# A hybrid attention and state-space layer on one core: convolution steps spread over the attention units, low parts of the weights on the vector engine, panels loaded a tile earlier

## The reference

```
proj  = RMSNorm(x) @ W_in              # q, k, v, forget logits, z, xBC, dt, two gates
att   = softmax(q k^T * scale + c_q - c_k, causal) v      # 16 heads x 64
xBC   = silu(causal convolution of width 4 over time (xBC) + bias)   # 4096 channels
y_ssm = Mamba-2 scan(xBC, dt) * silu(z), grouped RMSNorm
x     = x + (sigmoid(g_att) * (att @ W_pa) + sigmoid(g_ssm) * (y_ssm @ W_pb)) @ W_out
x     = x + relu(RMSNorm(x) @ W_up)^2 @ W_down
```

## Time and profile before

| what | value |
|---|---|
| median of 3 runs | 2886.76 us (2885.06 to 2887.47) |
| profiled execution | 2885.89 us, its span 2884.1 us |
| mean granted TensorE clock | 0.978 |
| PE busy | 2737.1 us, 95% |
| DVE busy | 1577.2 us, 55% |
| ACT busy | 1022.4 us, 35% |
| POOL busy | 405.7 us, 14% |

### The profile page before, as it was taken

How to read it: one execution, slowest core, us unless ns; L and a number is a source line. 1 busy time by engine, 2 the same in 40 slices (tenths; PEclk the granted TensorE clock), 3 DMA queues, 4 the chain that set the end, 5 groups by cost and what they waited for, 6 DMA issues and landing times. The chain is left out here.

```text
span 2884.1 us, 47789 instructions
## 1 busy us (share of the span) xinstructions
PE 2737.1 (95%) x18754; PEld 2658.0 (92%) x18754; DVE 1577.2 (55%) x2867; ACT 1022.4 (35%) x2353; POOL 405.7 (14%) x475
## 2 busy tenths in 40 slices
PE   6998979999999999997999989998989999999999
PEld 5997978989999889887999979998989999999999
DVE  4336337656566565565898864464373444434434
ACT  4223336556666655653434331121231111111110
POOL 0000012212122222222555520000000000000000
PEclk8999999999999999998999999999989999999999
DMA  3222232132232222215888873343221111111112
GB/s 115 90 90 53 79 90 91 43 101 76 67 108 76 66 93 58 84 63 140 205 194 214 201 203 121 112 134 128 65 99 58 45 44 45 44 45 44 48 67 96
DMA packets 334448, 273.31 MB, mean 95 GB/s; under 512 B 95952, under 2 KB 311632, under 8 KB 334096
## 3 DMA queue, kind: packets, MB, share of 16 engines
q1 hardware_dynamic: 334224, 270.25, 32.9%
HBM read 197.90 MB, written 72.28 MB: 94 GB/s over the span
## 5 line engine op out<-in xcount | busy, mean ns | idle before, releaser
L411 PE MATMUL banks<-w_hi,xn_hi 128*128 128x256 f32 x1440 | 407.8, 287 | 8.7 <-DVEq L368 5.0
L411 PE MATMUL banks<-w_lo,xn_hi 128*128 128x256 f32 x1440 | 405.5, 286 | 0.0
L414 PE MATMUL banks<-xn_hi,w_hi 128*128 128x352 f32 x1152 | 379.5, 329 | 0.7 <-ACT att_xs L986 0.7
L414 PE MATMUL banks<-xn_hi,w_lo 128*128 128x352 f32 x1152 | 378.7, 329 | 0.0
L414 PE MATMUL banks<-xn_lo,w_hi 128*128 128x352 f32 x1152 | 378.2, 328 | 0.0
L411 PE MATMUL banks<-w_hi,xn_lo 128*128 128x256 f32 x1280 | 366.3, 286 | 0.0
L411 PEld LDWEIGHTS banks<-w_hi,xn_hi 128*128 128x128 f32 x1440 | 276.7, 192 | 10.6 <-DVEq L368 5.1
L411 PEld LDWEIGHTS banks<-w_lo,xn_hi 128*128 128x128 f32 x1440 | 276.6, 192 | 0.2
L1704 PE MATMUL banks<-h_hi,w_hi 128*128 128x352 f32 x768 | 248.8, 324 | 1.9 <-DVEq L1625 1.9
L1704 PE MATMUL banks<-h_lo,w_hi 128*128 128x352 f32 x768 | 248.6, 324 | 0.0
L1704 PE MATMUL banks<-mlp_uhi,w_hi 128*128 128x352 f32 x768 | 248.6, 324 | 0.0
(11 more groups left out here) (293 smaller groups left out, 6160.8 us busy)
## 6 DMA issues: line engine op xcount, KB each, us to landing
w_raw<-in_w_in SPq DMA_DIRECT2D x44, 1024.0 KB, 5.5
scratch_xbc<-att_co SPq DMA_DIRECT2D x32, 512.0 KB, 2.6
ssd_ab<-scratch_acum SPq DMA_DIRECT2D x64, 256.0 KB, 6.0
br_g<-scratch_gates SPq DMA_DIRECT2D x72, 176.0 KB, 2.8
scratch_gates<-hand_tanh SPq DMA_DIRECT2D x48, 176.0 KB, 5.4
scratch_z<-att_z_stage SPq DMA_DIRECT2D x64, 128.0 KB, 1.9
ssd_xbc<-scratch_xbc SPq DMA_DIRECT2D x64, 128.0 KB, 3.4
ssd_xbc<-scratch_xbc SPq DMA_DIRECT2D x128, 64.0 KB, 3.7
```

What stands on the lines that cost most here:

```text
L411: ins = self.nc.tensor.matmul(self.bank(n, P, PW), x[:, k, t * P:(t + 1) * P], w[:, k, :], start=first, stop=end)
L414: ins = self.nc.tensor.matmul(self.bank(n, P, TT), w[:, k, m * P:(m + 1) * P], x[:, k, r * TT:(r + 1) * TT], start=first, stop=end)
```

## The change

1. load is called at tile 4 of a panel instead of tile 5, in every stream (all five stages that have one).
2. In attention_z_xbc the low parts of the weights are made by DVE, as in the other stages. POOL keeps its 80 copies of q and k, in one loop without the stream's parts.
3. ConvFm.dve no longer computes at the ends of tiles. It puts steps in a queue, four taps when a block ends and the last step five tiles later, and ConvFm.step takes one from its head. The units call step at three or four points each: after the first top_score of the unit, after the second, after the ends of slot 1, and after add_out. What is left of a block's taps four tiles after its end is done there at once. The tanh moves from four tiles after the block to five, the store from five to six.
4. In unit 2 the parts of the slots are 2, 2, 4 instead of 2, 3, 3.

```diff
-            self.split_lo(pool, self.nc.gpsimd, i, j + 1, t - 1)
-            pool.wait_ge(self.lo_made, 4 * (i * len(self.panels) + j + 1) + t)
...
     def sp(self, sp, i, n, last):
         j, t = self.tiles[n]
-        if t == 5:
+        if t == 4:
             self.load(sp, i, j + 2, last)
...
-        if 1 <= t < 5 and not self.low_on_pool:
-            self.split_lo(dve, self.nc.vector, i, j + 1, t - 1)
+        if 1 <= t < 5:
+            self.split_lo(dve, i, j + 1, t - 1)
...
     def dve(self, dve, i, n):          # ConvFm
+        for k, m in self.ended(n - 4):
+            while self.due and self.due[0][0] <= (i * self.per + k) * 2 + m:
+                self.step(dve)
+        for k, m in self.ended(n):
+            self.due += [((i * self.per + k) * 2 + m, j) for j in range(CW)]
         for k, m in self.ended(n - 5):
+            self.due += [((i * self.per + k) * 2 + m, CW)]
+
+    def step(self, dve):
+        if not self.due:
+            return
+        B, j = self.due.popleft()
+        m, co, xs = B % 2, self.co[B % 2][:], self.xs[B % 2]
+        if j == CW:
+            dve.wait_ge(self.tanhed, B + 1)
+            v.scalar_tensor_tensor(out=co, in0=self.tanh[:], scalar=1.0, in1=co, ...).then_inc(self.made, 1)
+            return
+        if j == 0:
+            dve.wait_ge(self.copied, 4 * B + 4)
+            dve.wait_ge(s.free, len(s.banks) + self.last_tile(B) + 1)
+            dve.wait_ge(self.stored[m], 32 * (B // 2 + 1))
+            v.tensor_scalar(co, xs[:, 0:L], ...).then_inc(self.chain, 1)
+        else:
+            dve.wait_ge(self.chain, 8 + 4 * B + j)
+            v.scalar_tensor_tensor(out=co, in0=xs[:, j:j + L], ..., in1=co, ...).then_inc(self.chain, 1)
...
-        share = {0: (3, 2, 1), 1: (3, 2, 1), 2: (2, 3, 3), 3: (2, 3, 1), 4: (2, 2, 1)}
+        share = {0: (3, 2, 1), 1: (3, 2, 1), 2: (2, 2, 4), 3: (2, 3, 1), 4: (2, 2, 1)}
...
             for x, (h, u) in enumerate(units):        # vector engine
...
                     probs_lo(h, u, 1)
+                xbc.step(dve)
                 if x:
                     tile_ends(*units[x - 1], 2)
                 tile_ends(h, u, 0)
...
                     top_score(hn, nxt[1])
+                    xbc.step(dve)
...
                 tile_ends(h, u, 1)
+                xbc.step(dve)
                 if not early(u) and len(nxt) == 2:
                     top_score(hn, nxt[1])
+                    xbc.step(dve)
...
                 add_out(x)
+                xbc.step(dve)
```

More of the change, by code:

```diff
@@ L14 @@
+from collections import deque
 from contextlib import ExitStack
@@ L277, in __init__ @@
         self.hi, self.lo = hi, lo
[L278 removed]
+        self.by_range = False
         self.running = [n for n, (j, t) in enumerate(self.tiles) if panels[j][0] and t == NT]
@@ L336, in split_hi, with split_lo @@
         self.nc.scalar.activation(self.whi[j % 2][:, q, :], self.raw[:, q, :], ACT.Copy).then_inc(self.hi_made, 1)
-    def split_lo(self, eng, ops, i, j, c):
+    def split_lo(self, dve, i, j, c):
         q = slice(c * KB // 4, (c + 1) * KB // 4)
-        eng.wait_ge(self.hi_made, 4 * (i * len(self.panels) + j) + c + 1)
-        ops.tensor_tensor(self.wlo[j % 2][:, q, :], self.raw[:, q, :],
-                          self.whi[j % 2][:, q, :].bitcast(F32), ALU.subtract).then_inc(self.lo_made, 1)
+        dve.wait_ge(self.hi_made, 4 * (i * len(self.panels) + j) + c + 1)
+        self.nc.vector.tensor_tensor(self.wlo[j % 2][:, q, :], self.raw[:, q, :],
+                                     self.whi[j % 2][:, q, :].bitcast(F32), ALU.subtract).then_inc(self.lo_made, 1)
     def start_sp(self, sp):
@@ L354, in start_act @@
             ep.start_act(act)
[L356 to L362, removed]
-            self.split_lo(pool, self.nc.gpsimd, i, j + 1, t - 1)
-            pool.wait_ge(self.lo_made, 4 * (i * len(self.panels) + j + 1) + t)
     def start_dve(self, dve):
-        if not self.low_on_pool:
-            dve.sem_inc(self.lo_made, 4)
+        dve.sem_inc(self.lo_made, 4)
         for ep in self.epilogues():
@@ L970, in act @@
         copy = s.nc.scalar.activation
-        for k, m in self.ended(n - 4):
+        for k, m in self.ended(n - 5):
             B = (i * self.per + k) * 2 + m
@@ L994, in dve @@
     def dve(self, dve, i, n):
[L995 to L1014, removed]
@@ L1015, in dve @@
-        for k, m in self.ended(n - 5):
-            B = (i * self.per + k) * 2 + m
-            dve.wait_ge(self.tanhed, B + 1)
-            s.nc.vector.scalar_tensor_tensor(out=self.co[m][:], in0=self.tanh[:], scalar=1.0, in1=self.co[m][:],
-                                             op0=ALU.add, op1=ALU.mult).then_inc(self.made, 1)
+        for k, m in self.ended(n - 4):
[3 more added lines that the diff above has]
+            self.due += [((i * self.per + k) * 2 + m, j) for j in range(CW)]
@@ new lines, in dve @@
+        for k, m in self.ended(n - 5):
+            self.due += [((i * self.per + k) * 2 + m, CW)]
+    def step(self, dve):
+        if not self.due:
+            return
+        s, v, NB, L = self.stream, self.stream.nc.vector, self.NB, self.L
+        B, j = self.due.popleft()
+        m, co, xs = B % 2, self.co[B % 2][:], self.xs[B % 2]
+        if j == CW:
+            dve.wait_ge(self.tanhed, B + 1)
+            v.scalar_tensor_tensor(out=co, in0=self.tanh[:], scalar=1.0, in1=co, op0=ALU.add, op1=ALU.mult).then_inc(self.made, 1)
+            return
[3 more added lines that the diff above has]
+            dve.wait_ge(self.stored[m], 32 * (B // 2 + 1))
+            v.tensor_scalar(co, xs[:, 0:L], self.taps[:, B:B + 1], self.past[:, B + (CW - 1) * NB:B + (CW - 1) * NB + 1],
+                            ALU.mult, ALU.add).then_inc(self.chain, 1)
+        else:
+            dve.wait_ge(self.chain, 8 + 4 * B + j)
+            v.scalar_tensor_tensor(out=co, in0=xs[:, j:j + L], scalar=self.taps[:, B + j * NB:B + j * NB + 1], in1=co,
+                                   op0=ALU.mult, op1=ALU.add).then_inc(self.chain, 1)
@@ L1021, in sp, with last_tile @@
+    def last_tile(self, B):
+        i, k, m = B // 2 // self.per, B // 2 % self.per, B % 2
+        s = self.stream
+        return i * s.slots + next(n for n, (j, t) in enumerate(s.tiles) if s.panels[j][2] is self and (s.panels[j][3], t) == (k, 3 * m + 2))
     def sp(self, sp, i, n):
-        for k, m in self.ended(n - 5):
+        for k, m in self.ended(n - 6):
             B = (i * self.per + k) * 2 + m
@@ L2166, in double @@
                     nc.gpsimd.tensor_copy(x[HD:P, :], x[0:HD, :].bitcast(F32)).then_inc(doubled, 1)
[L2167 to L2186, removed]
+            for h in range(H):
+                for g in SEQ:
+                    double(h, g)
         @block.vector
```

2 lines of the change are left out of this document (1 added, 1 removed).

## The result

The changed kernel takes 2913.03 us (median of 4 runs, 2907.31 to 2913.7) against 2886.88 us for the kernel before (4 runs, 2885.06 to 2887.47). The ratio is 1.0087 (95% interval 1.007 to 1.0105): 25 us slower, where 31 us faster was forecast. The time lies outside the range of 2841 to 2878 us. The profiled execution has a span of 2911.0 us.

A forecast was written before the change was run, and what follows sets the result against it. PE was taken as the bound, losing 48.35 us idle in attention, mostly to the softmax chain, plus half-rate clock. Gains of 41.8 less 11 lost give 31 us net: 2856 us from the median, range 2841 to 2878.

The forecast's parts named there:

- A new closeness: Attention: at 11 of 32 blocks the first tap waits for a store just issued; 9 us lost, bounds 0 and 35.
- Steps one at a time: Attention: one convolution step instead of four ahead of a maximum or reciprocal on DVE; 12 of 13.9 us gained.
- The clock: Five half-rate stretches, each at a stall, go with the stalls; 12 of 13.2 us gained, bounds 6 and 13.2.
- Unit 2 as 2, 2, 4: Ends of unit 2 in attention: one more part covers the chain behind the second score; 8 of 9.95 us gained.
- Loads at the fifth tile: Attention: all three ACT waits for late panels go; 9.85 us of PE stops gained, bounds 5 and 9.85.
- Low parts on DVE: Attention: 96 quarters put 71.4 us on DVE but mostly hide; 2 us of PE time lost, bounds -2 and +71.
- C: Rival: DVE becomes the bound in x panels and PE waits there; slower, some 2895 us, chance 0.09.
- A: Rival: the softmax chain is short anyway and ACT's queue is the next wait; 2873 us, chance 0.18.

The follow-up runs named there:

- a_tanh: Changed kernel with a block's last step written to the tanh buffer and stored from there, so the first tap waits for no store: 2878.48 us, ratio 0.9968.
- b_rest: Kernel before with low parts on DVE, load at tile 4 and store from the tanh buffer, without single steps or new unit 2 parts: ratio 0.9942.
- b_steps_tanh: Kernel before with the convolution's steps one at a time and the store from the tanh buffer: 2884.0 us, ratio 0.9982.
- b_lowdve: Kernel before with only the 96 low quarters of attention moved to DVE: 2883.76 us, ratio 0.9983.
- b_load4_low: Kernel before with loads at the fifth tile and low parts on DVE, the store as before: 2873.06 us, ratio 0.995.
- a_tanh_share: Changed kernel with the store from the tanh buffer and unit 2's parts back to 2, 3, 3: 2870.33 us, ratio 0.9943.
- b_tanh: Kernel before with only the last step written to the tanh buffer and stored from there: ratio 1.0.
- b_load4_tanh: Kernel before with loads at the fifth tile and the store from the tanh buffer, low parts still on POOL: 2886.19 us, ratio 0.9998.
- b_load4: Kernel before with only the panel load moved a tile earlier, to tile 4: 2885.87 us, ratio 0.9995.

## Why the prediction was wrong

The step that failed most is "A new closeness". Its place, its count (11 against 12) and its mean length (3.2 us against 3.1) were right; the term of 0.8 us of PE each, 9 us in all, was mis-sized. It is 2.9 us each, 34.3 us in all, at the upper bound of 35 that I had written beside it. Three things were left out. The forecast measured the wait against the parts that PE still had in x panels. Seven of the twelve waits are in z panels, and six of them stopped PE, 17.5 of the 25.7 us of stops behind the waits; of the five in x panels three did. Seven of the nine stops were followed by a half-rate stretch, as at 1059.5 us, and the clock is 13.7 of the 34.3 us; my clock term counted stretches that go and none that come. And SP issues the next head's loads at two of these places, so that the store is issued 3.9 us after the last step instead of 0.09. That the whole came out at the bound is in part chance: the bound has the wait in it and no clock, and what came is some 21 us of stops and 13.7 of clock.

*Steps one at a time.* I put 12 us of 13.9 as gone. In a_tanh the stops at the earlier trace rows and 1284.5 us are nearly gone and the one at 939.7 is halved (1.48 us). But the steps stand now behind the z step, behind add_out and ahead of unit 2's maximum, and without the store wait the balance is 0 (b_rest) to -5 us (b_steps_tanh). I had asked what stands ahead of a maximum where PE stopped, and not where it did not stop yet.

*The clock.* 12 us of gain were forecast. Without the store wait the half-rate stretches are 27.3 us (a_tanh) against 30.7: 1.7 us. With it they are 54.6, a loss of 12 us where a gain of 12 was forecast.

*Unit 2 as 2, 2, 4.* Forecast -8 us; +2.6 alone (the interval reaches -0.3) and +7 in a_tanh. I had named 2 us for a score that comes before the banks are free; the banks that were not free are the stream's.

*Loads at the fifth tile.* With the low parts on DVE the exp waits fall by 9.8 us, the 9.85 of the forecast. But the scaling waits grow by 3.6 and the half-rate stretches do not fall (20.5 us in b_lowdve, 27.3 in b_load4_low), so all in all it is 9.5 us, where the forecast had a share of the clock on top. Alone it is 1.4 us, since SP stands at the load until POOL's fourth quarter is made, and the store behind the load of 1 MB takes the gain. For SP's wait for DVE I had written under 2 us of the 5.5; no run measures this by itself, but with the quarters on DVE no panel came late.

*Low parts on DVE.* The 96 quarters took 68.0 us against 71.4 forecast, and the edit alone gains 4.9 us, beyond the bound of -2, where a cost of 2 us was forecast. More came back than I had counted. Groups by line in attention (count, busy, mean ns, idle before), first of the kernel before, then of the changed one:

```profile
L1018 DVE SCALAR_TENSOR_TENSOR att_co<-att_co_tanh,att_co 128x1059 f32<-128x1059 f32 x32 | 48.5, 1515 | 0.9
L846 DVE SCALAR_TENSOR_TENSOR att_z_stage<-att_z_tanh,att_z_stage 128x256 f32<-128x256 f32 x64 | 35.1, 552 | 29.0 <-ACT att_z_stage L837 28.6
L1010 DVE TENSOR_SCALAR att_co<-att_xs,att_taps,att_past_bias 128x1059 f32<-128x1059 f32 x32 | 29.6, 924 | 0.2
```

```profile
L1013 DVE SCALAR_TENSOR_TENSOR att_co<-att_xs,att_taps,att_co 128x1059 f32<-128x1059 f32 x96 | 125.9, 1312 | 0.5
L342 DVE TENSOR_TENSOR w_lo<-w_raw,w_hi 128x512 fp32r<-128x512 f32 x96 | 68.0, 713 | 0.3
L1003 DVE SCALAR_TENSOR_TENSOR att_co<-att_co_tanh,att_co 128x1059 f32<-128x1059 f32 x32 | 40.0, 1251 | 0.6 <-ACT att_co_tanh L966 0.5
L836 DVE SCALAR_TENSOR_TENSOR att_z_stage<-att_z_tanh,att_z_stage 128x256 f32<-128x256 f32 x64 | 26.6, 420 | 38.3 <-ACT att_z_stage L827 38.1
```

The taps fell from 1397 to 1312 ns (1320 forecast), but the last step from 1515 to 1251 and the z step from 552 to 420 too: 8.2, 8.5 and 8.5 us, and 3.1 us on the first tap. b_lowdve, where only the quarters moved, has the same means (1316, 1259, 419 and 823 ns), so it is POOL and not the new places of the steps. Of the 68 us put on DVE 28 came back, which leaves 40. By the earlier trace rows DVE is only 28 us busier, since that view counts overlapping ends of neighbours once; the forecast was 50 to 70.

The rule of the Trainium skill ("SBUF — State Buffer", section "Who interferes with whom") that the prediction weighed fits these rows: the instructions that gained have SBUF operands alone, and a maximum or a low part of the probabilities, which read a bank, kept their time (each group within 0.1 us in all). The first tap gained too, with one large input, of which the rule as the prediction told it says nothing. My reading of the earlier trace rows was too simple: the tap of 1.32 us also ran beside a POOL quarter, but it had started 0.36 us ahead of it, and the one of 2.34 us started 0.12 us behind the next. The risk that I took from the rule, quarters held up by POOL's copies, came, and is small. Eight of the 96 quarters took 1.10 us, each started beside a copy, where the median is 0.68; that is 3.4 us of DVE:

```profile
456.03 1.10 DVE L342 TENSOR_TENSOR w_lo<-w_raw,w_hi 128x512 fp32r<-128x512 f32 x1
...
455.45 1.14 POOL L2166 CAST att_k<-att_k 64x512 fp32r<-64x512 f32 x1 [14.40 <-ACT att_k L2059]
```

*The rivals.* C had the sign right and the store wait as one part of its price, but not its mechanism: DVE has idle time, the quarters hide, and most of the stop time behind the waits (17.5 of 25.7 us) is in z panels. A's thought, that what waits next comes at once, is nearer to what is left without the store wait: a_tanh gains 9.2 us. By the runs before, b_rest, a_tanh_share, a_tanh and the changed kernel the terms can be told one by one, each with its clock in it. Loads, quarters and the store from the tanh buffer gave 16.7 us where 7.8 was forecast; the steps 0 where 12 was; unit 2 cost 7.3 where a gain of 8 was; the store wait cost 34.3 where 9 was; and the 12 us of clock, forecast apart, are in none of them. These differences are 9 us the good way and 12, 15, 25 and 12 the bad, together some 56 us, the distance between forecast and result. In another order of the edits the terms would come out otherwise.

## What to carry to other kernels

A new wait on an engine that works in order is to be priced by what is queued behind it, not by who needs the waiting instruction. List every place where it falls, ask at each how much work PE still has, and add the clock of the stops that come. In this kernel the price was 0.7 to 0.9 us per us of wait, near my bound of 1 and not my likeliest value. Spreading work evenly over an engine takes it out of the few places where it hurt and puts it into all the others; list for each new place what stands behind it. When a step is moved, follow its DMA too: what SP has ahead of it, and which large transfer is in front of it. A buffer that is free at the right time, here the tanh buffer, takes away such a wait at no cost (b_tanh, ratio 1.0), as long as the store is not itself late: in b_load4_tanh ACT waits 7.1 us in DVE's place.

## What the runs showed of the hardware

A store issued close behind a large load takes here about as long as the load (6.0 us for the one at 1032.14). In b_load4 six stores of 512 KB that were issued 0.5 us behind a load of 1 MB took 6.5 to 6.7 us to land, against 2.6 us in the median before; in b_load4_low those that came 2.5 us behind it took 3.8 to 3.9 us. The reader at 1040.73 us in b_load4 started 8.1 us after the issue of its store.

VectorE is faster by more than a few per cent when GpSimd has little to do. In b_lowdve, where GpSimd's low parts are the only thing moved, the last step is 17% and the z step 24% faster.

The clock is a price of stops by itself, but not of each. In the changed kernel half-rate stretches stand behind stops of 1.95 and 1.61 us, ended at 1208.51 and 1222.71 us, as well as behind the long ones; in a_tanh a stop of 2.24 us, ended at 951.26, has none, and neither has the one of 3.15 us at 939.71 in the kernel before.
